# Norms without a stage of their own: the product stages sum the squares, the next stage scales the rows chunk by chunk

## The reference

```python
def rmsnorm(x, w):
    x32 = x.astype(jnp.float32)
    y = x32 * lax.rsqrt(jnp.mean(x32 * x32, axis=-1, keepdims=True) + EPS)
    return (y * w.astype(jnp.float32)).astype(x.dtype)

# first block, layer 0 and 1, then its final norm
h = h + pool_mixer(rmsnorm(h, norm_w[0]), ...)      # ends with (...) @ pool_w_out
h = h + hgrn2_mixer(rmsnorm(h, norm_w[1]), ...)     # ends with (...) @ hgrn_w_out
x = rmsnorm(h[:, N_META:], final_norm_w)
# second block: _rms_norm(x, g) * (1 + scale) + shift is the modulated norm
mod = silu(c) @ w_ada + b_ada                       # gives shift1, scale1, gate1, shift2, ...
h = _modulate(x, norm1_g, shift1, scale1)           # then h @ w_in, two attentions
x = x + gate1 * (o @ w_o)
h2 = _modulate(x, norm2_g, shift2, scale2)
x = x + gate2 * _peer(h2, w_pq, sub_keys, peer_u, peer_v)
```

## Time and profile before

| | us |
|---|---|
| median of the runs (lowest, highest) | 3195.02 (3191.38, 3195.83) |
| the profiled execution, its own time | 3190.77 |
| its span, first to last instruction | 3189.0 |
| pool_out, hgrn_out, attn_out | 124.1, 123.9, 55.0 |
| norm1 | 23.9 |
| gains, final and mod1 together | 35.6 |
| mod2 | 19.4 |
| peer, to the end | 1367.8 |

### The profile page before, as it was taken

The page is one execution under the profiler, slowest core; times in us unless marked ns, Lnnn a source line. Parts: engine busy times, 40 slices in busy tenths (PEclk is TensorE's granted clock), DMA queues, the critical chain, the costliest instruction groups (busy, mean ns, idle before and its releaser), DMA issues. The chain is left out here.

```text
span 3189.0 us, 36172 instructions
## 1 busy us (share of the span) xinstructions
PE 2524.9 (79%) x12276; PEld 1727.8 (54%) x12276; DVE 2174.3 (68%) x3964; ACT 995.8 (31%) x2010; POOL 1175.8 (37%) x952
## 2 busy tenths in 40 slices
PE   6998969999999867678798788876667676667666
PEld 5998959988888867234465543322222232223222
DVE  6356647877777776365543347788888788878876
ACT  2222146565555421223233212222222222222221
POOL 2343346555555431021000214443444444444442
PEclk8999979999999979878899899988988888888888
DMA  3232621111111054000110259999999999999998
GB/s 100 85 98 89 203 60 54 53 40 52 53 53 50 17 156 143 15 18 0 40 40 14 79 209 405 412 427 422 414 427 427 419 410 427 426 418 405 427 425 348
DMA packets 269758, 666.42 MB, mean 209 GB/s; under 512 B 13990, under 2 KB 201547, under 8 KB 203835
## 3 DMA queue, kind: packets, MB, share of 16 engines
q0 software_dynamic: 73728, 536.90, 40.3%
q1 hardware_dynamic: 194906, 127.75, 13.3%
q10 hardware_dynamic: 992, 0.13, 0.0%
HBM read 662.64 MB, written 2.10 MB: 208 GB/s over the span
## 5 line engine op out<-in xcount | busy, mean ns | idle before, releaser
L1900 PE MATMUL peer_py<-peer_uv,peer_diag 128*128 128x512 f32 x1536 | 850.0, 702 | 350.6 <-ACT peer_diag L1830 324.0
L1618 POOL DMA_INDIRECT peer_uv<-k_peer_uv,peer_idx x512 | 507.9, 992 | 774.2 <-PE peer_py L1900 713.0
L1900 PEld LDWEIGHTS peer_py<-peer_uv,peer_diag 128*128 128x128 f32 x1536 | 325.4, 224 | 840.7 <-issue 833.3
L1720 DVE SCALAR_TENSOR_TENSOR peer_spare<-peer_uv,peer_hp 128x1024 bf16<-128x1024 f32 x512 | 622.7, 1217 | 225.1 <-DMA peer_uv<-k_peer_uv,peer_idx 224.2
L1822 ACT ACTIVATE peer_ga<-peer_a 128x2 f32<-128x2 f32 x256 | 52.0, 203 | 826.4 <-DVE peer_spare L1720 826.3
L733 POOL TENSOR_TENSOR hgrn_wl<-p2n_w,hgrn_wh 128x1024 fp32r<-128x1024 f32 x64 | 158.6, 2488 | 269.6 <-ACT hgrn_wh L769 269.6
L862 PE MATMUL hgrn_pp<-p2n_hh,hgrn_wh 128*128 128x264 f32 x1024 | 220.2, 297 | 21.1 <-POOL hgrn_wl L733 21.1
L862 PE MATMUL hgrn_pp<-p2n_hl,hgrn_wh 128*128 128x264 f32 x1024 | 210.5, 287 | 0.0
L862 PE MATMUL hgrn_pp<-p2n_hh,hgrn_wl 128*128 128x264 f32 x1024 | 209.9, 287 | 0.0
L1830 ACT ACTIVATE peer_diag<-keep_ident,peer_wt 128x128 f32<-128x128 f32 x384 | 140.2, 396 | 114.4 <-DVE peer_wt L1727 109.0
L862 PEld LDWEIGHTS hgrn_pp<-p2n_hh,hgrn_wh 128*128 128x128 f32 x1024 | 161.7, 193 | 22.4 <-POOL hgrn_wl L733 21.9
(11 more groups left out here) (371 smaller groups left out, 4921.9 us busy)
## 6 DMA issues: line engine op xcount, KB each, us to landing
p2n_w<-in_hgrn_w_in SPq DMA_DIRECT2D x64, 512.0 KB
p1n_w<-in_pool_w_in SPq DMA_DIRECT2D x32, 512.0 KB
pool_out_aw<-in_w_ada SPq DMA_DIRECT2D x16, 768.0 KB, 4.7
hgrn_out_aw<-in_w_ada SPq DMA_DIRECT2D x16, 768.0 KB, 4.5
pool_out_w<-in_pool_w_out SPq DMA_DIRECT2D x8, 1024.0 KB, 6.9
hgrn_out_w<-in_hgrn_w_out SPq DMA_DIRECT2D x8, 1024.0 KB, 6.8
p_w<-in_w_pq SPq DMA_DIRECT2D x8, 1024.0 KB
peer_uv<-k_peer_uv,peer_idx POOLq DMA_INDIRECT x512
```

The costliest lines, as they stand in the source:

```text
L1618: pool.indirect_dma_start(out=uv[:, n % DEPTH].rearrange("p w d -> p (w d)"), out_offset=None, in_=io["k_peer_uv"], in_offset=bass.Indirec ...
L1720: dve.scalar_tensor_tensor(out=spare[:, n % 2, :], in0=uv[:, n % DEPTH, 0, :], scalar=1.0, in1=hp[:, t % 2, :], op0=ALU.mult, op1=ALU.mult ...
L1900: last = pe.matmul(py[:, h * 512:(h + 1) * 512], diag[:, products(n) % DIAGS, :], uv[:, n % DEPTH, 1, h * 512:(h + 1) * 512], start=n % (P ...
```

## The change

norm1, gains, final, mod1 and mod2 are no phases any more; norm0 stays. In a product phase ACT squares each finished block of 128 output features (`squares`), and DVE adds the square to a running sum `total` one step later (`add_squares`); hgrn_out keeps a second sum, of squares scaled by the final norm's weight. The next phase sums `total` over the partitions (`Norm` in hgrn and in peer; `NormPair` in latent, which gets both norms in one pass out of the two sums), takes root and reciprocal, scales chunk by chunk, and PE's first projection waits for each chunk by itself. In hgrn all eight low halves are made on POOL.

In the first step of a product phase PE multiplies all `wh`,`rh` pairs, then all `wl`,`rh`, then all `wh`,`rl`. Of `rl`, DVE makes 10 of 16 chunks (5 of 8) and POOL the rest, between its first and second `wl`. SP issues the weights of the step after next ahead of the `aw` blocks. The first weight block of hgrn_out is loaded at the start of hgrn, that of attn_out at the start of latent (`early`). The loads that stood in norm1, mod1 and mod2 now stand at the start of hgrn, latent and peer.

```diff
-def norm_phase(nc, name, x, out, gain, tokens, shift=None, halves=None, ahead=None):
+def norm_phase(nc, name, x, out, gain, tokens, shift=None, ahead=None):
...
+    def pe(self, pe):
+        half = self.tokens // 2
+        for h in range(2):
+            last = pe.matmul(self.sums[:, h, 0:half], self.keep["ones"][:, :], self.total[:, h * half:(h + 1) * half],
+                             start=True, stop=True)
+        last.then_inc(self.summed, 1)
...
+    def act(self, act):
+        act.activation(self.warm[:, :], self.keep["eps"][:, 0:1], ACT.Sqrt)
+        act.wait_ge(self.summed, 1)
+        act.activation(self.rs[:, :].rearrange("p (h t) -> p h t", h=2), self.sums[:, :, 0:self.tokens // 2], ACT.Sqrt,
+                       bias=self.keep["eps"][:, 0:1], scale=1.0 / D).then_inc(self.rooted, 1)
+        for c in range(KC):
+            act.wait_ge(self.scaled, c + 1)
+            if self.shift is not None:
+                act.activation(self.out[:, c, :], self.out[:, c, :], ACT.Identity, bias=self.shift(c))\
+                   .then_inc(self.ready, 1)
+            else:
+                act.activation(self.parts[0][:, c], self.out[:, c, :], ACT.Copy).then_inc(self.ready, 1)
+    def dve(self, dve):
+        dve.wait_ge(self.rooted, 1)
+        dve.reciprocal(self.rs[:, :], self.rs[:, :]).then_inc(self.own, 1)
+        dve.wait_ge(self.own, 1)
+        for c in range(KC):
+            dve.scalar_tensor_tensor(out=self.out[:, c, :], in0=self.x[:, c, 0:self.tokens], scalar=self.gain(c),
+                                     in1=self.rs[:, :], op0=ALU.mult, op1=ALU.mult).then_inc(self.scaled, 1)
+    def pool(self, pool):
+        if self.parts:
+            for c in range(KC):
+                pool.wait_ge(self.ready, c + 1)
+                pool.tensor_tensor(self.parts[1][:, c], self.out[:, c, :], self.parts[0][:, c].bitcast(F32), ALU.subtract)\
+                    .then_inc(self.low, 1)
...
+class NormPair:
...
+    def pe(self, pe):
+        for j, t in enumerate((self.total, self.weighted)):
+            pe.matmul(self.sums[:, j, :], self.keep["ones"][:, :], t[:, META:T], start=True, stop=True)\
+              .then_inc(self.summed, 1)
+    def act(self, act):
+        keep = self.keep
+        act.activation(self.warm[:, :], keep["eps"][:, 0:1], ACT.Sqrt)
+        act.wait_ge(self.summed, 1)
+        act.activation(self.ra[:, :], self.sums[:, 0, :], ACT.Sqrt, bias=keep["eps"][:, 0:1], scale=1.0 / D)\
+           .then_inc(self.rooted, 1)
+        act.wait_ge(self.scaled, 1)
+        act.activation(self.rb[:, :], self.rb[:, :], ACT.Sqrt, bias=keep["eps"][:, 0:1], scale=1.0 / D)\
+           .then_inc(self.rooted, 1)
+        for c in range(KC):
+            act.wait_ge(self.scaled, c + 2)
+            act.activation(self.out[:, c, :], self.out[:, c, :], ACT.Identity, bias=keep["mod"][:, c:c + 1])\
+               .then_inc(self.ready, 1)
+    def dve(self, dve):
+        keep = self.keep
...
+        at = COL["norm1_g_2"]
+        ch.link(dve.tensor_tensor(self.gains[:, :], self.weight, keep["cols"][:, at:at + KC], ALU.mult))
+        dve.wait_ge(self.rooted, 1)
+        ch.link(dve.reciprocal(self.ra[:, :], self.ra[:, :]))
+        dve.wait_ge(self.summed, 2)
+        ch.link(dve.tensor_tensor(self.rb[:, :], self.ra[:, :], self.sums[:, 1, :], ALU.mult))
+        dve.tensor_tensor(self.rb[:, :], self.rb[:, :], self.ra[:, :], ALU.mult).then_inc(self.scaled, 1)
+        dve.wait_ge(self.rooted, 2)
+        ch.link(dve.reciprocal(self.rb[:, :], self.rb[:, :]))
+        ch.link(dve.tensor_tensor(self.rab[:, :], self.ra[:, :], self.rb[:, :], ALU.mult))
+        for c in range(KC):
+            dve.scalar_tensor_tensor(out=self.out[:, c, :], in0=self.h[:, c, :], scalar=self.gains[:, c:c + 1],
+                                     in1=self.rab[:, :], op0=ALU.mult, op1=ALU.mult).then_inc(self.scaled, 1)
+    def residual(self, dve):
+        for c in range(KC):
+            dve.scalar_tensor_tensor(out=self.x[:, c, :], in0=self.h[:, c, :], scalar=self.weight[:, c:c + 1],
+                                     in1=self.ra[:, :], op0=ALU.mult, op1=ALU.mult)
...
+    by_dve = kc * 5 // 8
...
+            def weights(m, b):
                 sp.wait_ge(wl_done, m + 1)
+                sp.dma_start(w[b], view[:, :, ds(m * P, P)]).then_inc(w_in[b], 16)
+            def factors(m):
+                a_view = ada[0].rearrange("(k p) n -> p k n", p=P)
+                for h in range(2):
+                    sp.wait_ge(aw_used, m * 2 + (h + 1))
+                    sp.dma_start(aw[:, h], a_view[:, h * ak:(h + 1) * ak,
+                                                  ds((m + ada[1] * turns) * ADA_COLS, ADA_COLS)])\
+                      .then_inc(aw_in[h], 16)
+            if not early:
+                weights(0, 0)
+            weights(1, 1)
+            if ada:
+                factors(0)
+            with sp.Fori(0, turns // 2 - 1) as i:
+                for b in range(2):
+                    weights(i * 2 + (2 + b), b)
+                    if ada:
+                        factors(i * 2 + (1 + b))
+            if ada:
+                factors(turns - 1)
...
+                if first:
+                    pe.wait_ge(wh_done, 1)
+                    for j, (x, y) in enumerate(((wh, rh), (wl, rh), (wh, rl))):
+                        if j == 1:
+                            pe.wait_ge(wl_done, m + 3)
+                        for k in range(kc):
+                            if j == 0:
+                                pe.wait_ge(rh_done, k + 1)
+                            elif j == 2 and k < by_dve:
+                                pe.wait_ge(rl_done, k + 1)
+                            elif j == 2:
+                                pe.wait_ge(rl_done2, k - by_dve + 1)
+                            last = products(b, k, j, x, y)
...
+            def squares(m, b):
+                for j, (gain, total) in enumerate(totals):
+                    if j == 0:
+                        act.wait_ge(taken, (m + 3) * nsp)
+                        act.wait_ge(sq_added, (m + 1) * nt)
+                    act.activation(sq[:, j], target(m), ACT.Square, scale=gain(m) if gain else 1.0)\
+                       .then_inc(sq_done, 1)
...
+            low(0, 0)
+            for k in range(by_dve, kc):
+                pool.wait_ge(rh_done, k + 1)
+                pool.tensor_tensor(rl[:, k], rhs[:, k, 0:tokens], rh[:, k].bitcast(F32), ALU.subtract)\
+                    .then_inc(rl_done2, 1)
+            low(1, 1)
...
+            def add_squares(m):
+                for j, (gain, total) in enumerate(totals):
+                    dve.wait_ge(sq_done, m * nt + (j + 1))
+                    dve.wait_ge(sq_added, m * nt + (j + 1))
+                    dve.tensor_tensor(total[:, :], total[:, :], sq[:, j], ALU.add).then_inc(sq_added, 1)
...
+            norm.pool(pool)
...
             high(0, F)
             high(0, Q)
+            norm.act(act)
...
+                        pe.wait_ge(norm.low, c + 1)
...
+        norm = NormPair(keep, ph, keep["hT"][:, :, META:T], keep["xT"], hm, keep["total"], weighted, pr[:, 6:8, :])
...
+            ahead(sp)
...
+            norm.pe(pe)
...
+                        pe.wait_ge(norm.ready, k + 1)
...
+            norm.dve(dve)
+            norm.residual(dve)
...
+            for n in range(2):
+                load(sp, n, n)
...
+                        pe.wait_ge(norm.ready, c + 1)
...
+                    def hgrn_ahead(sp):
+                        view = io["hgrn_w_in"][0].rearrange("(k p) n -> p k n", p=P)
+                        for b, at in enumerate((E_IN, 0)):
+                            sp.dma_start(w[:, b], view[:, :, at:at + P]).then_inc(w_in[b], 16)
+                        sp.dma_start(masks[:, :, :], io["k_masks"]).then_inc(masks_in, 16)
+                        sp.dma_start(wo[:, :, :], io["hgrn_w_out"][0].rearrange("(k p) n -> p k n", p=P)[:, :, 0:P])\
+                          .then_inc(wo_in, 16)
+                    hgrn_phase(nc, io, keep, hh, hl, og, w, w_in, masks, masks_in, hgrn_ahead)
...
+                              early=(wo[:, :, :], wo_in), target=rows, totals=[(None, total), (final_weight, weighted)])
...
+                    def latent_ahead(sp):
+                        view = io["w_in_2"].rearrange("(k p) n -> p k n", p=P)
+                        sp.dma_start(w[:, :, :], view[:, :, 0:FQ_AT]).then_inc(w_in, 16)
+                        sp.dma_start(wo2[:, :, :], io["w_o_2"].rearrange("(k p) n -> p k n", p=P)[:, :, 0:P]).then_inc(wo2_in, 16)
+                        sp.dma_start(wf[:, :, :], view[:, :, FL_AT:IN_W]).then_inc(w_in, 16)
+                    latent_phase(nc, io, keep, hm, la, w, wf, w_in, weighted, latent_ahead)
...
+                product_phase(nc, "attn_out", io["w_o_2"], KC, oT, [(0, SEQ)], gated, keep, early=(wo2[:, :, :], wo2_in),
+                              target=rows2, totals=[(None, total[:, 0:SEQ])])
```

205 lines of the change are left out of this document (105 added, 100 removed).

## The result

The changed kernel takes 3165.32 us (median of 4 runs, 3162.74 to 3168.53) beside 3193.86 (4 runs, 3191.38 to 3195.83) for the kernel before: ratio 0.9912, 95% interval 0.9894 to 0.9929 (the 3195.02 of the table ahead of the prediction is the median of three of these four). It is faster, by 28.5 us or 0.9%, clear of the spread of the runs; 47 were forecast, and the time lies outside the range of 3137 to 3158.

The account below looks back on a forecast made before the run. Peer's DMA gathers end the chain, DVE bounds the norms and PE the product phases; the terms sum to -47.8 us, from 3190.8 to 3143.0, and the median 4.2 above gives 3147, range 3137 to 3158.

Parts of the forecast that it names:

- the fourth: Rival: weights issued at the stage starts land late, no longer under a norm; +7.5 us, 3155, chance 0.07.
- A: pool_out: the stall ahead of 330.28 goes, a wait of some 4.9 us in step 0 replaces it; -2.1 us.
- the third case: Rival: the clock stays up over the shorter stall in step 0; -3.7 us, 3143, chance 0.18.
- Case 2: Rival: DVE's burst is held, so A and the same in D give nothing; +4 us, 3151, chance 0.25.
- B: End of pool_out to hgrn's first gate: less norm and projection on the path, but load waits and slower chunks; -7.1 us.
- D: hgrn_out: resident first weights make step 0 5.2 us earlier, then -2.1 as in A; -7.3 us.
- the slower rival: DVE becomes the bound of the product steps, 16.6 us against PE's 12.4; +59 us, 3206, chance 0.02.
- E: hgrn_out to latent's projections: first matmul 20.1 us earlier, slower chunks give back 1.1; -19.0 us.
- F: mla and fox: no effect, 0.
- G: attn_out: resident first weights move ACT's first copy by 4.0 us, the split gives back 0.5; -3.5 us.
- H: End of attn_out to peer's projections: first matmul 9.6 us earlier, slower chunks give back 0.8; -8.8 us.
- C: hgrn: same work of 16 heads, masks and wo loaded behind the F and Q weights; 0.

Follow-up runs that it names:

- e1: The kernel before, with an unused tile of 64 bytes a partition ahead of peer's tiles; 3211.12 us against 3191.36, ratio 1.0057.
- e2: The changed kernel, with an unused tile of 192 bytes a partition ahead of peer's tiles; 3150.44 us, ratio 0.9868.
- e3: The changed kernel, with all low halves of the product phases' activations made on DVE, none on POOL; 3153.00 us, ratio 0.9877.
- e4: The changed kernel, with ACT in hgrn taking the norm's root ahead of the two weight copies; 3164.42 us, ratio 0.9910.
- e6: The changed kernel, with the first weights of hgrn_out and attn_out loaded in their own stage again; 3176.72 us in one run.
- e5: The kernel before, with an unused tile of 128 bytes a partition ahead of peer's tiles; 3208.95 us, ratio 1.0056.
- e9: The kernel before, with an unused tile of 32 bytes a partition ahead of peer's tiles; 3214.06 us, ratio 1.0061.
- e7: The changed kernel, with the order of SP's queue in the product stages as before, weights behind factors; 3191.18 us in one run.
- e8: The changed kernel with the edits of e2, e3 and e4 together; 3131.82 us, ratio 0.9811.
- e10: The kernel of e8, with DVE making every second low half of the normalised rows in hgrn; 3132.80 us, ratio 0.9805.

## Why the prediction was wrong, step by step

**The step that failed** is the first paragraph's: "the change touches only its first instructions, so whatever arrives earlier at peer's first matmul is passed on in full". The change moves all of peer's tiles by 2112 bytes, off the 256-byte boundary of the gather buffers, and peer is bound by the transfers into them. That is 18.1 us in the two traces, 19.8 in the time when it is done alone (e1) and 14.9 when it is undone (e2). The forecast of 3147 with these added is 3162 to 3167; 3165 was measured. With the boundary restored, the changed kernel takes 3150.44, inside the range. None of the rivals had it: the fourth looked for a transfer that becomes visible, not for one that becomes slower.

**A** (-2.1, measured -4.1, of which 0.7 came from ahead of the phase). The order of events was right to a microsecond: POOL's six in 1.73 us turns, `wl(1)` from about 308 to 313, DVE's tenth behind it, a wait of 4.9 forecast and 4.41 measured, step 1 at 315.6 and at 316.2. The term that was off is the 1.86 us for the fallen clock. The clock fell as forecast, but what it cost was paid in step 0, where the last 14 matmuls took 3.30 us instead of 1.85; it was back at 1.00 in step 1, which took 12.0 us (328.17 - 316.2) and not 14.24. So the time came out near the third case (chance 0.18), but its premise, a clock that stays up, did not hold. Why the clock came back sooner than behind the stall of 6.76 us is open. Case 2, the held burst, did not happen here; it came back in e3.

**B** (-7.1, measured -5.5). Mis-sized in four small places: Q's weights 1.8 us behind F's and not 1.3, the stage's start 3.97 us behind the last finish and not 3.25, 18.0 and not 17.7 from reciprocal to last half, and the gate 1.1 behind that and not 1.0. The order of ACT's queue held the root, as said; "about 6 us" of gain from another order was half wrong, since POOL then bounds (e4: 3.05).

**D** (-7.3, measured -8.6 behind hgrn's last row). Two parts: ACT's first copy came 5.0 us earlier behind hgrn's last row (5.2 forecast; e6, from the other side, puts the load at 6.4), and the exchange of stalls gave 3.6, as it gave 3.3 in A, where 2.1 was forecast for each. The steps stay at 12.3 us ((1228.69 - 1142.3)/7), so DVE does not become the bound, the slower rival.

**E** (-19.0, measured -16.6). The tail was 1.2 us longer, because the two squares and two adds follow the last finish one by one; the root waited for PE's two sums (2.2 us after the stage's start, not 1.5). And the handoff chunk by chunk cost PE nothing: a chunk comes each 0.67 us (5.36 for eight), while PE needed 10.2 us for eight chunks, from its first matmul at 1248.6 to the first projection, at a granted clock of 0.70, and 9.3 before, at 0.77. The 0.55 us per matmul taken from the earlier trace rows was half of one: the row counts two records for each matmul of 512 columns. The 1.1 us subtracted for the handoff were lost at the lower clock instead.

**F** (0, measured +5.1). latent's rest, mla and fox lost 5.1 us with unchanged code. Most of it is in mla; the stretch from the root of its first heads to that of its last took 144.1 instead of 141.1 us, before and after:

```profile
1368.10:1509.20 141.10, 108.23 (x364) 54.26 (x363) 93.43 (x107) 44.33 (x96) 27.56 (x24) 0.82 0.03 8
```

```profile
1335.90:1480.00 144.10, 113.18 (x364) 56.97 (x363) 93.39 (x107) 44.47 (x96) 27.59 (x24) 0.77 0.03 8
```

DVE's, ACT's and POOL's busy times agree within 0.2 us; PE's is 5.0 longer at a granted clock of 0.77 instead of 0.82. The same stretch took 141.0 to 141.3 in e1, e5, e9 and e3, 142.1 to 142.6 in e6, e7, e8 and e10, 144.2 in e2 and 146.3 in e4. The rows put the difference down to the clock. Where the tiles lie does not explain it, as it does the gathers: e3 has all its tiles where the changed kernel has them and the same code in hgrn, latent, mla and fox, and took 2.8 us less. Why the same code finds the clock lower in some kernels stays open.

**G** (-3.5, measured -3.1) and **H** (-8.8, measured -8.2) hold in size, though H took half of a matmul (0.61 us) for a whole one as E did; the loads that now start with the stages were covered, as worked out.

**C** (0, measured +1.3): hgrn from the first gate to its last row, unchanged code again.

In the two traces the 25.5 us are made up of 18.1 in peer's transfers and +8.1 in the other terms (+5.1 in F, +2.4 in E, +1.6 in B, +1.3 in C, +0.6 in H, +0.4 in G, -1.3 in D, -2.0 in A), 6.4 of that in code that is the same, less 0.7 behind the last gather. The medians miss by 18.3 only, because the forecast put the median 4.2 us above the profiled execution and here it lay 3.2 below it. That these 18.3 equal the 18.1 of the transfers is chance; by e1 and e2 the transfers are 15 to 20 of them. The range was too narrow because it was made of the terms' bounds alone: there was no term for what unchanged code does at other addresses or at another clock.

## What to carry to other kernels

A new tile moves every tile that is allocated behind it: look up where the buffers of the transfer-bound stage start, before and after, and keep them on a multiple of 256 bytes; here a tile of 2112 bytes cost some 18 us, nearly a third of the 59.6 that the change gains in e8, with the boundary restored. When work is moved to an idle engine, ask what stands behind it in that engine's queue: GpSimd's six low halves were cheap and the `wl` behind them was what the next step waited for. And a gain of less than some 3 us in an early stage can't be read from the time of this kernel, because unchanged stages differ by as much from kernel to kernel; compare the points of two traces, stage by stage.

## What the runs showed of the hardware

- Gathers of 8 KB a partition ran at 413 to 414 GB/s (1302 to 1305 us for 512 of them, four kernels) into buffers at a multiple of 256 bytes (67584, 69888), and at 407 to 409 GB/s (1320 to 1326 us, eight kernels) into 67616, 67648, 67712 and 69696.
- DVE and POOL took turns when both had work queued (six POOL operations, an estimated 1.17 us each by the size of `wl`'s 4.52, in 10.39 us, and `wl(1)` behind them in 4.96), but a POOL operation that came alone into a run of DVE's low halves waited for all of it: 8.51 us before, and 8.49 in e3. The Trainium skill's SBUF — State Buffer, "Who interferes with whom", calls the ports that the two share an exclusive lock, held for a whole instruction by whoever issues first (the latter it says of VectorE's two-port modes; of `tensor_tensor` with both inputs in SBUF, the operation here, it says that it contends with GpSimd's reads). The turns agree with it and the 8.51 us do not; what decides between the two patterns is open.
- Behind a wait of PE of 4.41 us the granted clock was 0.52 for 3.1 us and then 1.00 (step 1: 12.0 us); in the step behind a wait of 6.76 us it was 0.83 on the mean, and the step took 1.86 us more than the next.
